# Fourier front: x loaded once, modulation weights in twelve pieces, row products as four 32-column tiles

## What is computed

```python
def _modulate(h, shift, scale):
    return h * (1.0 + scale) + shift

def _fourier_mixer(h, w_out, b_out):
    b, s, _ = h.shape
    hf = h.astype(jnp.float32).reshape(b, s, FNET_GROUPS, D_MODEL // FNET_GROUPS)
    mixed = jnp.fft.fft2(hf, axes=(1, 3), norm='ortho').real
    mixed = mixed.reshape(b, s, D_MODEL).astype(h.dtype)
    return mixed @ w_out + b_out
...
        sh1, sc1, g1, sh2, sc2, g2 = jnp.split((silu_c @ ada_w[i] + ada_b[i])[:, None, :], 6, axis=-1)
        csh1, csc1, cg1, csh2, csc2, cg2 = jnp.split(silu_cc @ ada_w[i] + ada_b[i], 6, axis=-1)
        n_lat = _modulate(_rms_norm(h_lat, norm1_g[i]), sh1, sc1)
        n_ctx = _modulate(_rms_norm(h_ctx, norm1_g[i]), csh1, csc1) if need_ctx_in else None
```

## Time and profile before

| | us |
|---|---|
| three runs | 2689.35, 2690.03, 2692.37 (median 2690.03) |
| the profiled execution | span 2688.1 from the first to the last instruction; the median lies 1.93 above it |
| first product of the mixer on VectorE | at 51.19 |
| end of the mixer | at 249.75 |
| busy over the span | PE 2508.7 (93%), DVE 1389.3 (52%), ACT 854.5 (32%), POOL 573.6 (21%) |

### The profile page before, as it was taken

The page is one execution under the profiler, slowest core; times in us unless marked ns, Lnnn a source line. Parts: engine busy times, 40 slices in busy tenths (PEclk is TensorE's granted clock), DMA queues, the critical chain, the costliest instruction groups (busy, mean ns, idle before and its releaser), DMA issues. The chain is left out here.

```text
span 2688.1 us, 34456 instructions
## 1 busy us (share of the span) xinstructions
PE 2508.7 (93%) x12084; PEld 2001.7 (74%) x12084; DVE 1389.3 (52%) x2306; ACT 854.5 (32%) x1462; POOL 573.6 (21%) x402
## 2 busy tenths in 40 slices
PE   6998997999999999999949788887989999999999
PEld 2555884888888888888747576765758888888887
DVE  2543877444344443444487688884273434343444
ACT  3433216211121121211163388884052121212121
POOL 0111003211112121111110155562032222222220
PEclk8999998999999999999979899999989999999999
DMA  7434741010101011010111211102021111111111
GB/s 291 118 101 149 269 153 63 32 47 31 47 31 47 31 39 39 31 47 16 62 59 67 71 29 28 27 16 102 28 74 47 47 47 47 47 47 47 49 45 63
DMA packets 83576, 176.71 MB, mean 66 GB/s; under 512 B 37952, under 2 KB 53824, under 8 KB 75584
## 3 DMA queue, kind: packets, MB, share of 16 engines
q1 hardware_dynamic: 72352, 121.47, 13.3%
q0 software_dynamic: 9152, 44.05, 4.7%
q10 hardware_dynamic: 2016, 10.49, 1.0%
HBM read 163.40 MB, written 12.58 MB: 65 GB/s over the span
## 5 line engine op out<-in xcount | busy, mean ns | idle before, releaser
L967 DVE SCALAR_TENSOR_TENSOR ht<-l_yy_ps,mod,ht 128x512 f32<-128x512 f32 (+1 forms) x640 | 445.5, 697 | 310.0 <-PE l_yy_ps L50 309.4
L48 PE MATMUL l_z_ps<-nh,l_w1h 128*128 128x512 f32 (+1 forms) x1280 | 477.9, 373 | 13.6 <-DVE nl L55 12.8
L49 PE MATMUL l_z_ps<-nl,l_w1h 128*128 128x512 f32 (+1 forms) x1280 | 474.3, 371 | 0.0
L50 PE MATMUL l_z_ps<-nh,l_w1l 128*128 128x512 f32 (+1 forms) x1280 | 473.8, 370 | 0.0
L48 PE MATMUL l_yy_ps<-l_ah,l_w2h 128*128 128x512 f32 (+1 forms) x1280 | 471.6, 368 | 2.1 <-DVE l_al L55 2.1
L49 PE MATMUL l_yy_ps<-l_al,l_w2h 128*128 128x512 f32 (+1 forms) x1280 | 471.3, 368 | 0.0
L50 PE MATMUL l_yy_ps<-l_ah,l_w2l 128*128 128x512 f32 (+1 forms) x1280 | 471.2, 368 | 0.0
L948 DVE TENSOR_TENSOR l_sq<-l_rel 128x512 f32<-128x512 f32 x160 | 118.9, 743 | 569.6 <-ACT l_rel L859 569.5
L48 PEld LDWEIGHTS l_z_ps<-nh,l_w1h 128*128 128x128 f32 x1280 | 243.8, 190 | 61.2 <-DVE nl L55 16.4
L55 POOL TENSOR_TENSOR l_w2l<-l_w2f,l_w2h 128x2048 fp32r<-128x2048 f32 x32 | 147.3, 4604 | 624.0 <-ACT l_w2h L852 624.0
L55 POOL TENSOR_TENSOR l_w1l<-l_w1f,l_w1h 128x2048 fp32r<-128x2048 f32 x32 | 147.4, 4606 | 614.3 <-ACT l_w1h L847 614.3
(11 more groups left out here) (208 smaller groups left out, 3589.7 us busy)
## 6 DMA issues: line engine op xcount, KB each, us to landing
l_w1f<-w SPq DMA_DIRECT2D x32, 1024.0 KB, 4.8
l_w2f<-w SPq DMA_DIRECT2D x32, 1024.0 KB, 4.8
aw<-ada POOLq DMA_DIRECT2D x24, 1024.0 KB, 5.2
maw<-ada POOLq DMA_DIRECT2D x64, 256.0 KB, 3.1
ada_w<-ada SPq DMA_DIRECT2D x4, 2048.0 KB, 11.1
qb<-queries SPq DMA_DIRECT2D x64, 128.0 KB, 2.7
xt<-x ACTq DMA_DIRECT2D x8, 512.0 KB, 19.3
xg<-x SPq DMA_DIRECT2D x8, 512.0 KB, 4.1
```

The lines of the kernel that those rows point to most:

```text
L48: pe.matmul(out, lh, rh, start=first, stop=False)
L49: pe.matmul(out, lh, rl, start=False, stop=False)
L50: return pe.matmul(out, ll, rh, start=False, stop=last)
L967: dve.scalar_tensor_tensor(out=h, in0=y_ps[u % 4][:, 0:n], scalar=mod[:, layer, G2, m, v:v + 1], in1=h, op0=ALU.mult, op1=ALU.add).then_in ...
```

## The change

- The prologue loads no whole piece of `ada_w[0]` any more. For the front x and ctx are loaded once, into `xs`, which lies where `nh` will be, group by group, in runs of 1 KiB. Odd tiles go through SP's queue and even ones through ScalarE's; the tables, the identity and the first three units of `ada_w[0]` follow on SP's queue. VectorE makes both parts of the tables. No modulation is computed there.
- All twelve pieces of `ada_w[0]` go through the mixer, three a group. Pieces 0 to 3 are put together anew on the host, so that piece g holds shift and scale of group g alone. `modulation(g)` makes them just before they are used. A unit is now half a piece (1 MiB), in a ring of three buffers filled by SP's queue.
- A unit's row products run as four products with 32 columns of weights each (2 of them not zero), each into 32 rows of PSUM; so two units leave four partial sums of the two rows. `ada_columns` multiplies by `sel`, which adds the four.
- The loops are written out, and ScalarE now copies the rows (`ada_rows`) and the columns (`ada_mod`) of a piece at fixed places.

The core of the diff:

```diff
+def prologue(...):
+        with nc.Block() as block:
+            @block.sync
+            def _(sp):
+                sp.dma_start(vec[:], vecs).then_inc(s_small, 16)
+                for t in range(1, NT, 2):
+                    sp.dma_start(xs[:, :, t, :], tokens(t)).then_inc(s_x[t], 16)
+                for i in range(4):
+                    sp.dma_start(tabf[:, i], dft[i]).then_inc(s_tab[i], 16)
+                sp.dma_start(ident[:], eye).then_inc(s_id, 16)
+                for u in range(ADA_RING):
+                    sp.dma_start(aw[u][:], ada0[u // 2, :, 4 * (u % 2):4 * (u % 2) + 4, :]).then_inc(s_aw[u], 16)
...
+            @block.scalar
+            def _(act):
+                for t in range(0, NT, 2):
+                    act.dma_start(xs[:, :, t, :], tokens(t)).then_inc(s_x[t], 16)
...
+                for t in range(NT):
+                    act.wait_ge(s_x[t], 16)
+                    if t:
+                        act.wait_ge(s_ssq, t)
+                    act.activation(xsq[:], xs[:, :, t, :], ACT.Square, accum_out=ssq[:, t:t + 1]).then_inc(s_ssq, 1)
...
+            @block.vector
+            def _(dve):
...
+                for i in range(4):
+                    dve.wait_ge(s_tab[i], 16)
+                    dve.tensor_scalar_mul(tabh[:, i], tabf[:, i], 1.0).then_inc(s_th, 1)
+                    dve.wait_ge(s_th, i + 1)
+                    lo_part(dve, tabl[:, i], tabf[:, i], tabh[:, i]).then_inc(s_tl, 1)
+                dve.wait_ge(s_id, 16)
+                dve.reduce_sum(sel[:], ident[:].rearrange("p (j c) -> p c j", c=32)[:, 0:2, :], axis=AX.X)
+                dve.wait_ge(s_std, 1)
+                dve.reciprocal(rstd_tm[:], ssq[:]).then_inc(s_d, 1)
...
 def fnet_mix(...):
...
+            @block.sync
+            def _(sp):
+                for u in range(ADA_RING, UNITS):
+                    sp.wait_ge(s_unit, u + 1 - ADA_RING)
+                    sp.dma_start(aw[u % ADA_RING][:], ada0[u // 2, :, 4 * (u % 2):4 * (u % 2) + 4, :]).then_inc(s_aw[u % ADA_RING], 16)
...
+                prep(0, 0)
+                ada_rows(0)
+                prep(0, 1)
+                ada_mod(0)
+                for g in range(GR):
+                    sets(g, 0)
+                    if g + 1 < GR:
+                        prep(g + 1, 0)
+                    ada_rows(3 * g + 1)
+                    sets(g, 1)
+                    ada_mod(3 * g + 1)
+                    if g + 1 < GR:
+                        prep(g + 1, 1)
+                        ada_rows(3 * g + 2)
+                        ada_mod(3 * g + 2)
+                    y_out(g, 0)
+                    p = 3 * g + 3 if g + 1 < GR else PIECES - 1
+                    ada_rows(p)
+                    y_out(g, 1)
+                    ada_mod(p)
...
+                def modulation(g):
+                    cols = mcol[:, 8 * g:8 * g + 8].rearrange("p (s k v) -> p s k v", s=2, k=2)
...
+                    dve.wait_ge(s_mc, g + 1)
+                    for v in range(2):
+                        dve.tensor_tensor(mod[:, 0, 0:2, 2 * g:2 * g + 2, v], cols[:, :, :, v], bias, ALU.add).then_inc(s_mod, 1)
...
-                def ada(g, units):
-                    for q in units:
-                        piece, k = divmod(q, KC)
-                        pe.matmul(row_ps[0:2, :], svec[:, k, :], aw[q % RING][:], start=(k == 0), stop=(k == KC - 1)).then_inc(s_unit, 1)
+                def ada(u):
+                    p, h = divmod(u, 2)
+                    pe.wait_ge(s_aw[u % ADA_RING], 16 * (u // ADA_RING + 1))
+                    if h == 0 and p:
+                        pe.wait_ge(s_row, p)
+                    for j in range(4):
+                        last = pe.matmul(row_ps[32 * j:32 * j + 32, :], sv[:, 4 * h + j, :], aw[u % ADA_RING][:, j, :],
+                                         start=(h == 0), stop=(h == 1))
+                    last.then_inc(s_unit, 1)
...
-                        if per:
-                            ada(ada_g, range(q0 + j * per, q0 + (j + 1) * per))
+                        if j < 2:
+                            ada(2 * p + j)
+                    ada_columns(p)
...
-                        ada(g, (8, 9) if m == 0 else (14,))
+                        if m == 0:
+                            ada(2 * p)
+                        else:
+                            ada_columns(p)
...
-                        ada(g, (10, 11) if m == 0 else (15,))
+                        if m == 0:
+                            ada(2 * p + 1)
```

More of the change, by code:

```diff
@@ L99, in scale @@
             return mod[:, l, (SC1, SC2)[n], k, v:v + 1]
+        nh_at = -(-nc.sbuf_base // 32) * 32
         nh = sb("nh", [P, KC, T], F32R)
         nl = sb("nl", [P, KC, T], F32R)
[L104 to L118, removed]
@@ L243, in hybrid_kernel @@
-        fnet_mix(nc, sem, sb, banks, x, ctxt, xg, tabh, tabl, rstd_tm, ada0, vec, svec, ident, mod, g1b, nh, nl)
-        tables.close()
+        sv = sb("sv", [P, KC, 32])
+        with ExitStack() as front:
+            xs = nc.alloc_sbuf_tensor_at("xs", [P, GR, NT, GW], F32, offset=nh_at)
+            tabh = sb("tabh", [P, 4, 2, 512], F32R, where=front)
+            tabl = sb("tabl", [P, 4, 2, 512], F32R, where=front)
+            aw = [sb(f"maw{i}", [P, 4, PIECE], where=front) for i in range(ADA_RING)]
+            sel = sb("sel", [P, 2], where=front)
+            s_aw = [sem(f"m_aw{i}") for i in range(ADA_RING)]
+            prologue(nc, sem, sb, x, ctxt, vecs, ada0, dft, eye, vec, sv, svec, ident, sel, meanw, eps, ones, rstd_tm, xs, tabh, tabl, aw, s_aw)
+            fnet_mix(nc, sem, sb, banks, ada0, xs, tabh, tabl, rstd_tm, vec, sv, sel, mod, g1b, nh, nl, aw, s_aw)
@@ L290, in fnet_mix @@
         sdc = sb("sdc", [P, KC, 2], where=ph)
-        gain = sb("gain", [P, 2, 2], where=ph)
         yt = sb("yt", [P, 512], where=ph)
-        bt = sb("bt", [P, 256], where=ph)
-        RING = 4
-        UNITS = 2 * KC
-        aw = [sb(f"maw{i}", [P, PIECE], where=ph) for i in range(RING)]
-        rows = sb("mrows", [2, PIECE], where=ph)
+        bt = sd[:, 0:256]
+        rows = sb("mrows", [P, PIECE], where=ph)
+        mcol = sb("mcol", [P, 8 * PIECES], where=ph)
         seq_ps, y_banks = banks("seq_ps", 4, ph), banks("y_ps", 2, ph)
@@ L311, in fnet_mix @@
         s_y, s_bt, s_yt, s_yh, s_yl = sem("m_y"), sem("m_bt"), sem("m_yt"), sem("m_yh"), sem("m_yl")
-        xv = x.rearrange("(n p) d -> p n d", p=P)
-        cv = ctxt.rearrange("(n p) d -> p n d", p=P)
-        def schedule(eng, prep, sets, y_out):
-            prep(0, 0)
-            prep(0, 1)
-            with eng.Fori(0, GR - 1) as g:
-                for i in range(2):
-                    sets(g, i)
-                    prep(g + 1, i)
-                y_out(g)
-            for i in range(2):
-                sets(GR - 1, i)
-            y_out(GR - 1)
@@ L328, in fnet_mix @@
[L328 to L338 removed]
+        MODS = 8
@@ new lines, in _ @@
+                prep(0, 0)
+                prep(0, 1)
+                modulation(0)
+                for g in range(GR):
+                    sets(g, 0)
+                    if g + 1 < GR:
+                        prep(g + 1, 0)
+                    sets(g, 1)
+                    if g + 1 < GR:
+                        prep(g + 1, 1)
+                        modulation(g + 1)
+                    for m in range(2):
+                        y_out(g, m)
+                dve.wait_ge(s_mc, PIECES)
@@ L1753 @@
     pieces = a["ada_w"].reshape(DEPTH, KC, P, 6 * D // PIECE, PIECE).transpose(0, 3, 2, 1, 4)
+    pairs = a["ada_w"][0][:, :2 * D].reshape(KC, P, 2, GR, GW).transpose(3, 1, 0, 2, 4).reshape(GR, P, KC, PIECE)
+    first = np.concatenate([pairs, pieces[0, GR:]])
     both = pieces[1, 0:4].reshape(4, P, 2, 4 * PIECE).transpose(0, 2, 1, 3)
@@ L1759 @@
         "x": a["x"][0], "ctx": a["ctx"][0], "vecs": vecs,
-        "ada0": pieces[0], "ada1": units,
+        "ada0": first, "ada1": units,
         "w1": a["mlp_w1"].reshape(DEPTH, KC, P, DFF // (2 * P), 2 * P).transpose(0, 3, 2, 1, 4),
```

370 lines of the change are left out of this document (136 added, 234 removed).

## The result

The changed kernel takes **2646.78 us** (median of 4 runs, 2646.01 to 2649.51) against 2690.0 for the kernel before in the same measurement: ratio 0.984, 95% interval 0.9826 to 0.9854. That is 43.2 us less, where the forecast had 26; the time lies inside the range (2640 to 2681). The profiled execution has a span of 2644.3 us (before 2688.1, -43.8).

A forecast was written before the change was run, and what follows sets the result against it. Transfers and then VectorE's table conversions were taken to end the prologue, TensorE to bound the mixer. Terms -25.5 - 7.7 + 4.2 + 2.2 + 1 = -25.8 took the span from 2688.1 to 2662.3, median 2664 us; range 2640 to 2681.

The forecast's parts named there:

- the likeliest case: Mixer row products as a staircase, only neighbouring tiles' passes overlapping, 2.33 us a unit; 2664 us in all, chance 0.53.
- the row products, 24 x 2.33 = 55.9: TensorE in the mixer: 24 units of 2.33 us replace 63.6 us of row products, -7.7 us.
- all four at once: Rival for the mixer's row products: four tiles run together, unit 1.04 us, VectorE and ScalarE set the pace; 2645, chance 0.22.
- Prologue, -25.5: Before the mixer: first product at 25.7 us instead of 51.19, at 402 GB/s; bounds 24.5 and 30.
- Columns +4.2: TensorE's column steps in the mixer: eight pieces become twelve at 1.04 us each, +4.2 us.
- modulation(0) +2.2: Mixer start: modulation(0) must end before the first set leaves PSUM, so TensorE's next set waits, +2.2 us.
- Last group +1: Mixer's last group: without units stretching the token sums, feature sums wait for VectorE's last low part, +1 us.
- Between groups 0: TensorE's idle time between mixer groups: columns move away, the copies that end the wait stay, 0 us.
- Serial: Rival for the mixer's row products: tiles one after the other, 3.62 us a unit, 2695, or 2718 with weight loads; chance 0.19.
- A change of tiling mode: Argument within the serial rival: switching tiling drains TensorE, 48 times in this change, with no price given.
- The slow clock spreads: Rival: a new wait inside a mixer group lowers TensorE's clock, 3.4 us a group at most, up to 2678; no separate chance.
- I carry the rest over at its old length: Everything behind the mixer is unchanged, so its length was taken as before.

The follow-up runs named there:

- rows_early: Changed kernel with ScalarE's copy of the rows of piece 3g+2 moved ahead of the next group's second-half gh conversion; 2644.71 us.
- long_runs: Changed kernel with every tile of x landing on chip as one piece of 4 KiB a row instead of four of 1 KiB; 2647.38 us.
- one_tile: Changed kernel with all four products of a unit sent to the same 32 columns of the array and added up there; 2701.91 us.

## Why the prediction was right, and where it was wrong

- **Direction and range held**, but the time is that of the rival with 0.22, not of the likeliest case. Two terms were off, in opposite senses.
- **The term that failed is the row products, 24 x 2.33 = 55.9.** The step behind it was that "the second pass of a tile can overlap only with the first pass of the next". It took the order of whole passes from rows in which one product runs at a time. Measured are 1.00 us from the unit's first start to the next token sum (91.70 to 92.70), which with the same break ahead (0.32 less 0.23 of spacing) makes 1.09, and 24 x 1.09 = 26.2: 29.7 us less than forecast. Some 23 of these came out as time. The others went, roughly, into waits beyond the 3.2 forecast (about 4 of the 7.3 more idle time), into TensorE's other products, which took 2.6 longer, and into the 2.0 more between TensorE's last matmul and the mixer's end (2.73 now, 0.69 before).
- **The rival "all four at once" was right in the units and close in the numbers**: period 40.8, measured 40.93; TensorE idle ahead of the columns behind ScalarE's rows copy, measured 4.6 us; 2645, measured 2646.78. Its chain is not the one that binds. It ran through the second half's `gh` and the rows copy to the feature sums; but the columns ahead of them start without a wait in the later groups, and rows_early, with that copy out of the way, has periods of 40.97 and 40.94. What binds is the first half's `gl` and then TensorE's work, a chain of nearly the same length. That the time came within 2 us is in part luck as well: its mixer was to be 19.5 us shorter (45.0 less the prologue's 25.5) and is 23.1 shorter, 3.6 more, which offsets a prologue 2.2 and a rest 2.5 too short in the forecast. The Trainium skill, "TensorE: Matmul & The Clock Gate", Part 3, gives some 4 ns of issue for each further tile of a packed group. Here four first passes start within 40 ns, and four tiles cost 1.06 where one product costs 1.04. That part's sentence that matmuls start and end in program order cannot be read of whole two-pass products here: the second pass of the first product starts behind the first pass of the fourth.
- **Prologue, -25.5: measured -23.3.** The table's high part took 0.69 (forecast 0.72). The first table came at 19.88 and not 16.9, 3.0 late; the four tables took 7.5 in place of 8.0. The rate was wrong: 402 GB/s were carried over from runs of another length, 351 came, and long_runs shows that this is the 1-KiB runs, 1.7 of the 3.0 us. In the rest lie the first microseconds (149 GB/s from 2 to 3, 290 from 3 to 4) and the 0.4 for completion, which no row shows. The bound of 30 took it in, the likeliest value did not; but 640 KiB in 3.6 us, from which the bound has its 2 us, are 182 GB/s with issue and completion in them, and do not give that number.
- **Columns +4.2**: 11.8 - 8.4 = +3.4. **modulation(0) +2.2**: 1.85. **Last group +1**: 1.70 against 0.6 before. **Between groups 0**: the three waits for `uvf` rose from 3.4 to 5.0 us (the fourth of the 6.8 is modulation(0)'s), those for the rows copy from 1.9 to 4.6. The latter are TensorE arriving earlier: in one_tile they are gone. The former are not: in one_tile, where TensorE sets the pace, the four make 7.6; why they grew was not looked into.
- **"Serial"** was excluded by the trace, and its price was right: one_tile's unit is the 3.62 of the forecast, and the kernel is then slower than before, at 2701.9 where the forecast gave 2695.
- **A change of tiling mode** (the drain of the other rival): from the last token sum to the first pass of a unit are 0.32 us (91.38 to 91.70), as before without tiles (67.31 to 67.63). No price shows.
- **"The slow clock spreads"**: it did not. Over TensorE's time in the mixer the granted clock is 0.95, before 0.96.
- **"I carry the rest over at its old length"**: 2.5 us longer in the profile, with slow clock that comes and goes. This step was good to a few us and no better.

## What to carry over

Small products that fill few columns of the array are worth putting into separate column tiles, also when each takes two passes: here four products then cost what one does. Work out at once, stretch by stretch, which engine sets the pace when TensorE's load falls, because that gives the gain: a unit made shorter wins its full price only where TensorE does not wait for others. And do not read a wait's last releaser as its cause: move it and see whether the wait takes another name. The rate of a load differed with its run length here (351 and 411 GB/s); take it from a row with that length.

## What had not been expected

- Two-pass products in different column tiles run pass by pass together: 2, 4 and 8 passes in 1.04, 1.91 and 3.62 us as one product, two tiles with two each and one tile with four.
- x in runs of 1 KiB came at 351 GB/s, in runs of 4 KiB at 411, with the DMA engines full in both (share 1.09 and 1.02).
- Code that no edit touched took from 2437.7 to 2447.8 us. Some 3 us of this lie in its first 50 us, 4 to 7 some 1250 us further on, and in both places the long profiles are those with the lower granted clock; what lowers it is open.
